# Results of expert items weighted where they leave PSUM, and added into the residual rows by the DMA

## What is computed

```python
def moe_swiglu(x, w_router, b_router, w_g, w_u, w_d):
    logits = x @ w_router + b_router
    top_v, top_i = lax.top_k(logits, 2)          # two of eight experts for each token
    top_w = jax.nn.softmax(top_v, axis=-1)
    combine = sum(one_hot(top_i, 8) * top_w)     # the weight of each expert for each token
    y = sum over e of combine[e] * ((silu(x @ w_g[e]) * (x @ w_u[e])) @ w_d[e])
...
    x = layer_norm(ALPHA * x + moe_swiglu(x, ...), ln2_g, ln2_b)
```

## Time and profile before

| what | value |
|---|---|
| median of three runs (range) | 1646.91 us (1645.08 to 1647.98) |
| the profiled execution, its own time | 1647.25 us |
| span of its profile | 1645.4 us |
| granted TensorE clock, mean | 0.988 |
| item 0, items 1 to 9, final item | from 1066.9, 1125, 1568 us |

### The profile page before, as it was taken

The page is one execution under the profiler, slowest core; times in us unless marked ns, Lnnn a source line. Parts: engine busy times, 40 slices in busy tenths (PEclk is TensorE's granted clock), DMA queues, the critical chain, the costliest instruction groups (busy, mean ns, idle before and its releaser), DMA issues.

```text
span 1645.4 us, 20013 instructions
## 1 busy us (share of the span) xinstructions
PE 1584.4 (96%) x7315; PEld 1264.9 (77%) x7315; DVE 1151.2 (70%) x1339; ACT 807.4 (49%) x1095; POOL 170.1 (10%) x112
## 2 busy tenths in 40 slices
PE   7999999999999999999999999789999999999993
PEld 7877777888888888888777778567777777777772
DVE  6888846584434333288888574789888888888886
ACT  5344442252322222253444422557777777777763
POOL 0410005142000000004100051100000000000030
PEclk9999999999999999999999999899999999999997
DMA  5222222325454332212222235199999999999993
GB/s 211 77 91 76 77 102 90 103 76 202 145 201 144 102 122 96 101 66 77 100 67 77 77 115 206 64 397 392 384 372 381 370 371 372 375 372 381 375 337 142
DMA packets 133521, 324.52 MB, mean 197 GB/s; under 512 B 8188, under 2 KB 19836, under 8 KB 132944
## 3 DMA queue, kind: packets, MB, share of 16 engines
q1 hardware_dynamic: 124432, 290.27, 49.5%
q0 software_dynamic: 5872, 21.84, 3.5%
q10 hardware_dynamic: 3152, 11.54, 1.8%
HBM read 297.06 MB, written 27.26 MB: 197 GB/s over the span
## 4 chain that ended last, share of the span: by engine, by line
PE 91%; DVE 4%; issue 2%; ACT 1%; DMA 1%; POOL 1%; ACTq 0%; SPq 0%; DVEq 0%; POOLq 0%
PE bank L1464 15%; PE bank L1465 15%; PE bank L1466 15%; PE bank L1749 8%; PE bank L1751 8%; PE bank L1750 8%; PE bank L1503 4%; PE bank L1504 4%; PE bank L1502 4%; PE bank L1757 3%; PE bank L1728 1%; DVE ewlo L1104 1%; PE bank L1576 1%; PE bank L1589 1%; PE bank L1561 1%
## 5 line engine op out<-in xcount | busy, mean ns | idle before, releaser
L880 DVE TENSOR_TENSOR wlo<-raw,whi 128x1024 fp32r<-128x1024 f32 x170 | 238.9, 1408 | 207.7 <-ACT whi L554 207.4
L1464 PE MATMUL bank<-xth,whi 128*128 128x512 f32 (+1 forms) x976 | 381.5, 391 | 1.7 <-DVE wlo L880 1.7
L1465 PE MATMUL bank<-xtl,whi 128*128 128x512 f32 (+1 forms) x976 | 370.9, 380 | 0.0
L1466 PE MATMUL bank<-xth,wlo 128*128 128x512 f32 (+1 forms) x976 | 370.6, 380 | 0.0
L1104 DVE TENSOR_TENSOR ewlo<-eraw,ewhi 128x2048 fp32r<-128x2048 f32 x132 | 302.0, 2289 | 62.5 <-ACT ewhi L749 62.5
L749 ACT ACTIVATE ewhi<-eraw 128x2048 fp32r<-128x2048 f32 x132 | 252.2, 1911 | 42.8 <-PE bank L1751 42.8
L554 ACT ACTIVATE whi<-raw 128x1024 fp32r<-128x1024 f32 x170 | 178.5, 1051 | 137.0 <-PE bank L1504 123.9
L1464 PEld LDWEIGHTS bank<-xth,whi 128*128 128x128 f32 x976 | 184.3, 189 | 50.5 <-issue 8.5
L1465 PEld LDWEIGHTS bank<-xtl,whi 128*128 128x128 f32 x976 | 184.3, 189 | 36.8 <-issue 3.8
L1466 PEld LDWEIGHTS bank<-xth,wlo 128*128 128x128 f32 x976 | 184.1, 189 | 35.2
L1749 PE MATMUL bank<-ewhi,xgh 128*128 128x512 f32 (+1 forms) x528 | 205.9, 390 | 4.6 <-DVE xgl L1190 2.8
(11 more groups left out here) (280 smaller groups left out, 2229.2 us busy)
## 6 DMA issues: line engine op xcount, KB each, us to landing
eraw<-expert_gu SPq DMA_DIRECT2D x99, 1024.0 KB, 8.2
raw<-dense_w SPq DMA_DIRECT2D x170, 512.0 KB, 3.5
eraw<-expert_dn SPq DMA_DIRECT2D x33, 1024.0 KB, 8.0
erawx<-expert_gu SPq DMA_DIRECT2D x22, 1024.0 KB, 8.2
eplain<-expert_dn SPq DMA_DIRECT2D x22, 768.0 KB, 10.1
erawx<-expert_dn SPq DMA_DIRECT2D x11, 1024.0 KB, 9.1
item_rows<-zero POOLq DMA_DIRECT2D x8, 1024.0 KB, 4.8
rows<-item_rows ACTq DMA_DIRECT2D x10, 512.0 KB, 7.1
```

What stands on the lines that cost most here:

```text
L880: V.tensor_tensor(wlo[:, g % SPL, :], raw[:, g % RAW, :], whi[:, g % SPL, :], ALU.subtract).then_inc(lo_done, 1)
L1464: mm(out, wh, xh, start=first, stop=False)
L1465: mm(out, wh, xl, start=False, stop=False)
L1466: return mm(out, wl, xh, start=False, stop=last)
```

## The change

The final item's four small matmuls and their operations go. In their place GpSimd writes a table, one line of 64 bytes for each slot (weight, token, a one), into unused rows of `xd`: eight indirect DMAs behind the scatter of `X`, from `about`, which VectorE fills in `slot_info` behind piece 5 of item 0. ScalarE loads an item's 128 lines (`load_info`) at p = 9 of each item, in the final one at p = 2; before the first load of each item it waits for the whole table (`info_out`). `y_out` multiplies by the slot's weight while it leaves PSUM. So the results in `yd` are weighted, and the gathers add them straight into `X` by DMA (`compute_op=ALU.add`), all four tiles for k = 0, then for k = 1. A slot of the final item is gathered from a zero row. `add_rest` goes. `residual_base` moves: four operations to the end of item 0, four to the end of item 1, where `rest_rows` finds the rows to gather. `last_slots` moves from item 0 to the end of the final item. In the closing layer norm `affine_out(0)` stands ahead of `scale_rows(0)`.

```diff
+INFO = 16
+INFO_ROW = MAX_ITEMS * CAP * (D // INFO)
...
+        about = at("about", [P, 2, TT, INFO], F32, o_ends)
+        info = at("info", [P, INFO], F32)
...
-        ybuf = [rows[:, :], xg32[:, :, :].rearrange("p k n -> p (k n)"), yrows[:, :]]
+        zs = yrows[:, :]
+        info_rows = xd.rearrange("r (a b) -> (r a) b", b=INFO)
...
@@ SyncE, at the end
             for tt in range(TT):
-                sp.wait_ge(y_added, 2 * tt + 2)
+                sp.wait_ge(gathered[tt], 32)
                 sp.dma_start(xd[tt * P:(tt + 1) * P], X[:, tt, :]).then_inc(z_stored, 16)
@@ ScalarE
+            def load_info(j):
+                act.dma_start(info[:, :], info_rows[bass.ds(j * CAP + INFO_ROW, CAP)]).then_inc(in_info, 16)
...
                 if h == 0:
                     act.wait_ge(e_out, j * 16 + 16)
-                nc.scalar.activation(yrows[:, 512 * h:512 * h + 512], bank[B_Y[h]][:, :], ACT.Copy).then_inc(e_y, 1)
+                    act.wait_ge(in_info, j * 16 + 16)
+                nc.scalar.activation(yrows[:, 512 * h:512 * h + 512], bank[B_Y[h]][:, :], ACT.Copy,
+                                     scale=info[:, 0:1]).then_inc(e_y, 1)
...
                     if p == 3:
                         act.wait_ge(scattered, 16 * 2 * TT)
                         load_rows(j + 1)
+                    if p == 9:
+                        act.wait_ge(info_out, 16 * 2 * TT)
+                        load_info(j)
...
                 if p == 2:
 
+                    load_info(final)
                     act.wait_ge(e_out, final * 16 + 16)
-                    act.wait_ge(rows_tr, final * 2 + 2)
-                    act.wait_ge(xg_lo, final * 2 + 2)
                     nc.scalar.activation(begun[:, :], eps[:, 0:1], ACT.Copy).then_inc(rows_free, 1)
...
-                act.wait_ge(y_added, 2 * tt + 2)
+                act.wait_ge(gathered[tt], 32)
@@ VectorE: L1169 to L1184 (dist, place, wlast, wrest, sel_last) are dropped
+            def slot_info():
+
+                V.tensor_copy(about[:, :, :, 0], mixk[:, :, :])
+                V.tensor_copy(about[:, :, :, 1], cst[:, C_TOK:C_TOK + TT].unsqueeze(1).broadcast_to([P, 2, TT]))
+                V.memset(about[:, :, :, 2:INFO], 1.0)
+                step(V.tensor_scalar(irow[:, :, :], rowk[:, :, :], float(INFO_ROW), None, ALU.add))
+                V.tensor_copy(iidx[:, :, :], irow[:, :, :]).then_inc(rt_info, 1)
+
+            def rest_rows():
+
+                step(V.tensor_scalar(lastb[:, :], end[:, 7:8], float(CAP), -float(CAP), ALU.mult, ALU.add))
+                step(V.tensor_scalar(inl[:, :, :], rowk[:, :, :], lastb[:, 0:1], None, ALU.is_ge))
+                step(V.tensor_scalar(grow[:, :, :], rowk[:, :, :], -1.0, float(N_ROWS - 1), ALU.mult, ALU.add))
+                step(V.tensor_tensor(grow[:, :, :], grow[:, :, :], inl[:, :, :], ALU.mult))
+                step(V.tensor_tensor(grow[:, :, :], grow[:, :, :], rowk[:, :, :], ALU.add))
+                V.tensor_copy(gidx[:, :, :], grow[:, :, :]).then_inc(rt_slots, 1)
...
                     e_low(p + ESPL, j)
-                    if first and p >= 6:
-                        residual_base(p - 6)
+                    if begun == 0 and p == 5:
+                        slot_info()
                 e_low(14, j)
-                if first:
-                    for i in range(5, 8):
+                if begun < 2:
+                    for i in range(4 * begun, 4 * begun + 4):
                         residual_base(i)
-                    last_slots()
+                if begun == 1:
+                    rest_rows()
...
-            dve.wait_ge(about_mm, 1)
-            step(V.tensor_copy(mslot[:, :], bank[7][:, 0:4]))
-            item(0, True)
-            with dve.Fori(1, final) as j:
+            item(0, 0)
+            item(1, 1)
+            with dve.Fori(2, final) as j:
                 item(j)
...
                 e_low(p + ESPL, final)
-                if p >= 5:
-                    add_rest(p - 5)
             e_low(14, final)
-            add_rest(6)
-            add_rest(7)
+            last_slots()
...
-            dve.wait_ge(y_added, 2 * TT)
+            dve.wait_ge(gathered[TT - 1], 32)
             spread(0, X[:, TT - 1, :])
             turn_std(0)
-            dve.wait_ge(z_stored, 16 * TT)
-            scale_rows(0, X[:, TT - 1, :]).then_inc(out_pool, 1)
             affine_out(0)
+            scale_rows(0, X[:, TT - 1, :], z_stored).then_inc(out_pool, 1)
@@ GpSimd
+            pool.wait_ge(rt_info, 1)
+            for tt in range(TT):
+                for k in range(2):
+                    pool.indirect_dma_start(out=info_rows, out_offset=bass.IndirectOffsetOnAxis(
+                        ap=iidx[:, k, tt:tt + 1], axis=0), in_=about[:, k, tt, :], in_offset=None).then_inc(info_out, 16)
+
             pool.wait_ge(x_base, TT)
+            pool.wait_ge(rt_slots, 1)
             pool.dma_start(lngb[:, :, :], lnrow[3:4].broadcast_to([P, 2, D])).then_inc(in_ln3, 16)
             pool.wait_ge(rows_free, 1)
-            for g in range(2 * TT):
-                if g >= 3:
-                    pool.wait_ge(y_added, g - 2)
-                pool.indirect_dma_start(out=ybuf[g % 3], out_offset=None, in_=yd,
-                                        in_offset=bass.IndirectOffsetOnAxis(ap=gidx[:, g % 2, g // 2:g // 2 + 1], axis=0)
-                                        ).then_inc(gathered[g % 3], 16)
-            pool.wait_ge(rt_slots, 1)
-            pool.wait_ge(y_added, 2 * TT)
+            for k in range(2):
+                for tt in range(TT):
+                    if k == 1:
+                        pool.wait_ge(gathered[tt], 16)
+                    pool.indirect_dma_start(out=X[:, tt, :], out_offset=None, in_=yd,
+                                            in_offset=bass.IndirectOffsetOnAxis(ap=gidx[:, k, tt:tt + 1], axis=0),
+                                            compute_op=ALU.add).then_inc(gathered[tt], 16)
+            pool.wait_ge(rt_slots, 2)
             pool.wait_ge(z_stored, 16 * TT)
...
@@ TensorE
             turn_rows()
-            pe.wait_ge(rt_last, 1)
-            for tt in range(TT):
-                ins = mm(bank[7][:, 0:4], sel_last[:, tt, :], about[:, tt, :], start=(tt == 0), stop=(tt == TT - 1))
-            ins.then_inc(about_mm, 1)
```

More of the change, by code:

```diff
@@ L267, in build_trunk @@
         tab = at("tab", [P, 32], I32)
+        o_ends = here()
         ends = at("ends", [P, 16, NE], F32)
-        o_sel = here()
         sel = at("sel", [P, TT, CAP], F32R)
-        sel_last = at("sel_last", [P, TT, CAP], F32, o_sel)
         ones16 = at("ones16", [P, 2, P], BF16)
@@ L274, in build_trunk @@
         lastb = at("lastb", [P, 1], F32)
-        dist = at("dist", [P, 2, TT], F32)
         inl = at("inl", [P, 2, TT], F32)
-        place = at("place", [P, TT], F32)
-        wlast = at("wlast", [P, 2, TT], F32)
-        wrest = at("wrest", [P, 2, TT], F32)
         grow = at("grow", [P, 2, TT], F32)
         gidx = at("gidx", [P, 2, TT], U32)
-        about = at("about", [P, TT, 4], F32)
-        mslot = at("mslot", [P, 4], F32)
+        irow = at("irow", [P, 2, TT], F32)
+        iidx = at("iidx", [P, 2, TT], U32)
+        about = at("about", [P, 2, TT, INFO], F32, o_ends)
+        info = at("info", [P, INFO], F32)
         skip = at("skip", [P, 4], F32)
@@ L362, in build_trunk @@
         e_y, e_out = sem("e_y"), sem("e_out")
-        gathered = [sem(f"gathered{i}") for i in range(3)]
+        gathered = [sem(f"gathered{tt}") for tt in range(TT)]
         out_done = sem("out_done")
         y_ready, last_ready, last_done = sem("y_ready"), sem("last_ready"), sem("last_done")
-        rt_last, about_mm, rt_slots = sem("rt_last"), sem("about_mm"), sem("rt_slots")
-        y_added, z_stored, base_in = sem("y_added"), sem("z_stored"), sem("base_in")
+        rt_info, info_out, in_info, rt_slots = sem("rt_info"), sem("info_out"), sem("in_info"), sem("rt_slots")
+        z_stored, base_in = sem("z_stored"), sem("base_in")
         sum_done, mean_done, out_sd = sem("sum_done"), sem("mean_done"), sem("out_sd")
@@ L1167, in _ @@
             step(V.tensor_tensor(mixk[:, 1, :], etmp[:, 1, :], mixk[:, 0, :], ALU.mult))
[L1169 to L1181, removed]
-            for tt in range(TT):
-                ins = V.tensor_scalar(sel_last[:, tt, :], slot_no[:, :], place[:, tt:tt + 1], None, ALU.is_equal)
-            ins.then_inc(rt_last, 1)
+            def slot_info():
[11 more added lines that the diff above has]
+                V.tensor_copy(gidx[:, :, :], grow[:, :, :]).then_inc(rt_slots, 1)
             def xg_low(j):
@@ L1224, in last_slots @@
             def last_slots():
-                tok, valid = mslot[:, 0:1], mslot[:, 2:3]
+                dve.wait_ge(in_info, final * 16 + 16)
+                tok, valid = info[:, 1:2], info[:, 2:3]
                 V.tensor_scalar(skip[:, 0:1], valid, -float(SKIP), float(SKIP), ALU.mult, ALU.add)
@@ L1234, in last_slots, with item @@
```

(13 more changed lines are left out.)

5 lines of the change are left out of this document (2 added, 3 removed).

## The result

The changed kernel takes 1660.84 us in the median of four runs (1658.93 to 1661.69), the kernel before on the same chip 1646.41 (1645.08 to 1647.98). The ratio is 1.0084, interval 1.0072 to 1.0097: slower by 14.4 us, where I had forecast 2.9.

A forecast was written before the change was run, and what follows sets the result against it. TensorE was read as busy for 96% of the span, the end as set by the last store of `X`. Against 1647.25 us, + 10.4 + 0.5 - 8.0 = + 2.9 gave 1650.2, as median 1649.8; range 1641 to 1658.5.

The forecast's parts named there:

- Routing: Ahead of item 0, the small matmuls, `sel_last` and their operations go: taken as 0, at most 0.94 us gained.
- Item 0: ScalarE's wait for the table at p = 9 and the half clock after it: 10.4 us lost, 8.4 to 17.9.
- Rival A: Item 0: GpSimd isn't held up by VectorE, table there at 1107.5; sum 1641.5 to 1644.2 us; chance 0.23.
- The landing: Item 0: the table's 8 KB DMA taken to land 3.0 us after issue, with 1 and 10.5 us as ends.
- Rival C: Item 0: the table's small lines land 10.5 us after the last issue, 7.5 us more, 1657; chance 0.10.
- (a): Stretch from the start of item 0 to the final item's first tanh: forecast +10.9 us on 506.15.
- Item 1's end: Residual operations and `rest_rows` add 6.1 us to VectorE where it idles 7.1: taken as 0, 2 us at most.
- The final item: Last gather landed at 1607.0, first normalisation moved from 1618.0 to 1610.0: 8.0 us gained.
- extra pass: Final item: an adding gather takes one more pass over its 512 KB at 399 GB/s, 1.4 us.
- (b): Stretch from the final item's first tanh to the first normalisation: forecast -8.0 us on 45.0.
- Rival B: Final item: adding gathers are slow and follow each other, 4 us each; time 1658; chance 0.13.
- The stretch behind it: From the first normalisation to the end of the span: the 27.4 us stay, change 0.

The follow-up runs named there:

- e2: The changed kernel with the table's lines filled in the routing, before item 0, instead of behind its piece 5: 1645.29 us, ratio 0.9986 to the kernel before.
- e4: The kernel before with only the residual operations moved, four to the end of item 0 and four to the end of item 1: 1642.88 us, ratio 0.9975.
- e3: The changed kernel with the last gathers released only behind the final item's last split, when the weights have landed: 1677.17 us, ratio 1.0179 to the kernel before.
- e1: The changed kernel with the eight last gathers as plain copies into X instead of additions: 1651.63 us, ratio 1.003 to the kernel before.
- e6: The changed kernel with the table filled early and all eight last gathers plain, added by VectorE: 1642.64 us, ratio 0.9975 to the kernel before.
- e7: The changed kernel with ScalarE's table wait and load moved from p = 9 to behind the item's last hidden block: 1653.79 us, ratio 1.0037 to the kernel before.
- e5: The changed kernel, table early, four last gathers (k = 0) adding by DMA, four plain ones added by VectorE: 1641.19 us, ratio 0.9966 to the kernel before.
- e8: e5 with the order turned, four plain gathers first and the four adding ones last: 1641.05 us, ratio 0.9956 to the kernel before.

## Why the prediction was wrong

**Routing: right.** I took 0. From the transposes of item 0's own rows to its first matmul on weights there are 5.87 us after (1062.03 to 1067.90). Before, the same transposes (L1699) stood at 1061.00 and item 0 began 5.88 us later: the 0.94 us went into the next wait, 4.79 instead of 2.80. The 1.0 us by which item 0 starts later had been there by then; in the eight experiments that start lies between 1065.9 and 1068.9, in no order of what was changed.

**Item 0: right in its steps, and in its sum partly by luck.** GpSimd began at 1095.1 (forecast 1094.8 at the earliest). Three DMAs were held by VectorE, and the last was out at 1110.4 (forecast 1109.8, between 1109.2 and 1110.4). Rival A fell with that, and the trace after again disagrees with the inference that it rested on (the Trainium skill, "SBUF — State Buffer", "Who interferes with whom"): issues of 2.6 to 3.1 us inside `tensor_tensor`, 0.95 outside. The landing was larger than taken: about 1114.7, 4.3 us after the last issue for the 3.0 I took. Rival C's 10.5 did not come. The clock fell to 0.50, as forecast. All items together lost 10.5 us for the 10.9 forecast. e2 and e4 show its two parts: the wait costs 15.4 us, where I had counted 13.9 (7.7 + 3.5 + 2.7), and the residual operations' move gains 5.0, where I had counted 3.5. The two errors of 1.5 us cancel, and that the sum came so near is luck. The nine `load_info` cost next to nothing: e2, which has them, and e4, which hasn't, differ by 0.1 us in (a).

**Item 1's end: right.** The moved operations show no wait of TensorE there, and e4 gains in (a) all the same.

**The final item: wrong, and this is the step that failed.** "I take one more pass over the 512 KB at 399 GB/s, 1.4 us", and from that "landed at 1607.0", "8.0 us gained". (512 KB at 399 GB/s are 1.3 us, which changes nothing.) GpSimd's pace was right: the last gather was out 29.7 us after the first tanh, forecast 29.0. The extra pass by itself was nearly right too, 1.2 us of the engines by e3. Wrong was where I charged it: once, to the landing of the last gather. The engines were full already (share 1.04; 1.03 in e1's final item, with plain gathers), so all eight take their extra time from everything that is under way in the same engines: the weights, the gathers themselves, and the stores of `X` that follow. I had the landing at 5.0 us behind the last issue (3.6 + 1.4), and it took 11.0; I had the store and its release at the 3.0 us of before, and they took 6.9. Of the 10.5 us between forecast (37.0) and measured (47.5) in (b):

- 7.7 us are the addition, 9.1 (e1) less the 1.4 that I charged. It comes out at two places: the last gather landed 40.6 us after the first tanh, 5.5 later than e1's, and the first normalisation stands 6.9 us behind that landing instead of e1's 3.3. Two things hold it there and end within 0.1 us of each other: the last store, and ScalarE's statistics behind the weights of 1625.1. e2, with the weights 6 us earlier and still 6.0 us from landing to normalisation, shows that the store alone is enough.
- 2.9 us are left without the addition (e1's 38.4 against 37.0 - 1.4). Nearly all of that is landing: e1's last gather landed 6.1 us after it was out, I had taken the 3.6 of a transfer without other traffic.

Rival B had the cause in part, slow additions that follow each other, and the nearest time (1658). Its price isn't quite what happened: the gathers were issued 2.9 us apart, set by VectorE, and landed 3.3 us apart (the four stores that the last four landings release start at 1615.2 to 1625.2), not 4; and B left the store at its old price.

**The stretch behind it: 0.4 us off.** I took 0. It is 27.8 us in every run that has the change's closing layer norm and 27.4 in the two that haven't (before and e4). Which part of it costs the 0.4 was not tested.

**What the result means for the parts.** The change is several changes, and they go different ways: weights at the evacuation cost nothing that shows (e2 and e4 differ by 0.1 us in (a)), moving the residual operations gains 5.0 us, filling the table in item 0 loses 15.4, and adding all by DMA loses 1.8 to 3.2 against adding by VectorE (46.1 in e2 and 47.5 after against 44.3 in e6).

**Still open.** Whether the doubled time of the engines is the reading of the target or the addition itself: no row tells the two apart. And why the same load of weights, issued at the same distance from the first tanh, lands after 29.8 us in after and 29.2 in e7, but after 23.4 in e2.

## What to carry to other kernels

A DMA on full engines costs its time to everyone beside it: before pricing it by its own landing, read the DMA share of the stage, and ask which loads and stores it pushes back and who waits for them. A late load that an engine waits for need not be what sets the end: look at every wait that the last step has, since two can end together. A wait on an engine that works in order is paid by all that is queued there, and moving it changes who pays (e7: 6.3 us less, and 4.3 still lost); producing the data earlier removed it (e2). An indirect DMA on GpSimd that begins while VectorE runs a long operation on two SBUF operands took 2.4 to 3.1 us here instead of 0.95; that matters where someone waits for the last one.

## What the hardware showed unexpectedly

- A gather that adds fills the DMA engines at 211 to 213 GB/s (e3), a plain one with weights beside it at 398 (e1). Issued without VectorE beside it, it costs GpSimd 1.53 to 1.56 us, a plain one 0.94. It lands 10.3 us after its issue even with the weights out of the way, with up to four under way; before, plain ones among the weights took 7.0.
- Eight additions made one load of 1 MB land after 29.8 us instead of e1's 12.8, or after 23.4 (e2). With four of them issued first it took 23.1 us (e5), with four issued last 14.4 (e8).
- Eight indirect DMAs of 128 lines of 64 bytes, 8 KB each, had landed 4.3 us after the last was out, while the engines moved 392 GB/s (1110 to 1112 us) and 375 (1112 to 1114).
